# Alternating 512-column and 256-column products in a TensorE-bound fp32r transformer kernel

## The reference, cut to what matters

```python
proj = jnp.einsum('bsd,dc->bsc', x, w_in[layer])
...
h = jnp.square(jax.nn.relu(jnp.einsum('bsd,df->bsf', x, w_ff1[layer])))
y = jnp.einsum('bsf,fd->bsd', h, w_ff2[layer])
...
a, b = jnp.split(x @ w_in, 2, axis=-1)
return (jax.nn.silu(a) * b) @ w_out
...
y_g = o_g.reshape(B, S, GDN_WIDTH_V) @ w_branch_gdn
```

## Time and profile before

| | |
|---|---|
| median of 3 runs | 1370.94 us (1370.84 to 1371.84) |
| span of the profiled execution | 1369.8 us |
| granted clock of TensorE, mean | 0.999 of full speed |
| matmuls, each with a weight load | 8592 |
| read from memory | 225.90 MB, 166 GB/s over the span |

### The profile page before, as it was taken

One profiled execution on the slowest core, in us unless ns is written; L12 is line 12 of the kernel. 1 busy time (PEld: TensorE's weight loads), 2 busy tenths in 40 slices (PEclk: granted clock), 3 DMA queues, 4 the chain that ended last, 5 costly groups with the idle time before them and its releaser, 6 DMA issues.

```text
span 1369.8 us, 24310 instructions
## 1 busy us (share of the span) xinstructions
PE 1355.6 (99%) x8592; PEld 1211.1 (88%) x8592; DVE 1045.3 (76%) x1622; ACT 801.3 (58%) x1310; POOL 23.3 (2%) x71
## 2 busy tenths in 40 slices
PE   8999999999999999999999999999999999999998
PEld 8888888989888888888899999999999998988886
DVE  5798888777666686666778888888888877666665
ACT  4445554644443364444668898898898853544444
POOL 6000000000000000000000000000000000000000
PEclk9999999999999999999999999999999999999999
DMA  8565554655556746666574453554543286666661
GB/s 265 153 193 155 150 147 153 201 196 190 184 191 197 226 137 202 184 184 186 153 199 117 131 154 99 146 144 112 141 130 122 82 213 203 173 207 197 187 184 62
DMA packets 291214, 227.80 MB, mean 166 GB/s; under 512 B 10882, under 2 KB 270164, under 8 KB 291156
## 3 DMA queue, kind: packets, MB, share of 16 engines
q1 hardware_dynamic: 291012, 226.75, 55.6%
q10 hardware_dynamic: 144, 0.26, 0.1%
HBM read 225.90 MB, written 1.08 MB: 166 GB/s over the span
## 4 chain that ended last, share of the span: by engine, by line
PE 93%; DVE 3%; ACT 1%; DVEq 1%; issue 1%; DMA 1%; ACTq 0%; SPq 0%
PE M L2066 10%; PE G L2066 9%; PE M L2054 7%; PE M L2055 7%; PE M L2056 7%; PE G L2049 5%; PE M L2068 5%; PE G L2051 5%; PE G L2050 5%; PE G L2068 5%; PE G L2188 2%; PE G L2940 2%; PE M L2749 1%; PE M L2767 1%; PE G L2054 1%; PE G L2056 1%
## 5 line engine op out<-in xcount | busy, mean ns | idle before, releaser
L1203 DVE TENSOR_TENSOR w_lo<-w_raw,w_hi 128x2048 fp32r<-128x2048 f32 (+2 forms) x249 | 481.3, 1936 | 132.4 <-ACT w_hi L647 128.1
L647 ACT ACTIVATE w_hi<-w_raw 128x2048 fp32r<-128x2048 f32 x198 | 377.9, 1909 | 169.4 <-PE M L2068 54.3
L2049 PE MATMUL G<-xa,w_hi 128*128 128x256 f32 x592 | 176.8, 299 | 0.0
L2051 PE MATMUL G<-xa,w_lo 128*128 128x256 f32 x592 | 167.2, 282 | 0.0
L2050 PE MATMUL G<-xa,w_hi 128*128 128x256 f32 x592 | 167.0, 282 | 0.0
L2066 PE MATMUL M<-xa,w_hi 128*128 128x512 f32 x600 | 151.5, 394 | 0.0
L2066 PE MATMUL G<-xa,w_hi 128*128 128x512 f32 x568 | 142.5, 393 | 0.0
L2066 PEld LDWEIGHTS M<-xa,w_hi 128*128 128x128 f32 x600 | 107.8, 189 | 19.8
L2066 PEld LDWEIGHTS G<-xa,w_hi 128*128 128x128 f32 x568 | 104.0, 188 | 21.3 <-issue 1.2
L2054 PE MATMUL M<-w_hi,xb 128*128 128x512 f32 x300 | 117.3, 391 | 0.0
L2055 PE MATMUL M<-w_lo,xb 128*128 128x512 f32 x300 | 117.1, 390 | 0.0
(11 more groups left out here) (446 smaller groups left out, 2540.6 us busy)
## 6 DMA issues: line engine op xcount, KB each, us to landing
w_raw<-in_w_in SPq DMA_DIRECT2D x150, 512.0 KB, 4.7
w_raw<-in_ffn_w_in SPq DMA_DIRECT2D x88, 512.0 KB, 5.1
w_raw<-in_w_ff SPq DMA_DIRECT2D x64, 512.0 KB, 4.2
w_raw<-in_ffn_w_out SPq DMA_DIRECT2D x44, 512.0 KB, 5.0
w_raw<-in_w_in SPq DMA_DIRECT2D x33, 256.0 KB, 3.2
w_raw<-in_w_out SPq DMA_DIRECT2D x16, 512.0 KB, 4.0
w_raw<-in_w_branch_gdn SPq DMA_DIRECT2D x16, 512.0 KB, 5.3
w_raw<-in_w_branch SPq DMA_DIRECT2D x12, 512.0 KB, 4.2
```

Source lines behind the costliest of these rows:

```text
L647: nc.scalar.activation(w_hi[:, slot, :], w_raw[:, slot, :], ACT.Copy).then_inc(hi_ready, 1)
L1203: return v.tensor_tensor(dst, src, hi.bitcast(F32), ALU.subtract)
L2049: mm(out_, w[0], x[0], start=first, stop=False)
L2051: return mm(out_, w[1], x[0], start=False, stop=last_)
```

## The change

In both places the second loop over the k-tiles goes, and its product moves into the first loop. For each k-tile, the 512-column product with `w_hi` is followed at once by the 256-column product with `w_lo`. The operands, the banks, the start and stop flags and the signal on the last product are the same.

```diff
@@ -2064,7 +2064,6 @@
                 both_parts = bank.rearrange("p (h t) -> p h t", h=2)
                 for k in range(KT):
                     mm(both_parts, wh[:, k, at:at + P], xa[:, :, k, :], start=k == 0, stop=False)
-                for k in range(KT):
                     ins = mm(bank[:, 0:T], wl[:, k, at:at + P], xa_hi[:, k, :], start=False, stop=k == KT - 1)
             ins.then_inc(gemm_done, 1)
@@ -2938,7 +2937,6 @@
             wl_ = w_lo[:, c % RING, :].rearrange("p (k c) -> p k c", c=P)
             for k in range(16):
                 mm(G[:, n % 2, :].rearrange("p (h t) -> p h t", h=2), wh[:, k, :], xb[:, :, k, :], start=k == 0, stop=False)
-            for k in range(16):
                 ins = mm(G[:, n % 2, 0:T], wl_[:, k, :], xb_hi[:, k, :], start=False, stop=k == 15)
             ins.then_inc(gemm_done, 1)
```

## The result

The changed kernel takes 1377.08 us (median of four runs, 1376.63 to 1377.52) against 1371.15 for the kernel before on the same chip: a ratio of 1.0043, with an interval of 1.0031 to 1.0055. It is slower by 6 us, twice what a measurement can just tell apart. The profiled span went from 1369.8 to 1375.8 us, at the same granted clock of 0.999.

A forecast was written before the change was run, and what follows sets the result against it. TensorE's matmul stream was taken as the bound. Gains of 2.28, 0 and 0.15 us made 2.4, less 0.4 lost in the attention loop: 2.0 us, giving 1368.9 us; range 1362 to 1376, the forecast's own 1367 to 1370.

The forecast's parts named there:

- the price of the pair: TensorE's stream: a 512- and a 256-column product in turn cost their steady prices, 226.7+120 = 346.7 ns.
- 32 x 0: Groups of eight pairs directly behind 512-column products, 32 of 146: alternation gains nothing, 2.77 us either way.
- 8 x -19: Eight sixteen-pair groups of lines 2940/2942: 5.547 us instead of 5.566, a gain of 19 ns each.
- long groups: The eight sixteen-pair groups of lines 2940/2942, expected to read 5.55 us each after the change.
- 114: Groups of eight pairs not directly behind 512s: 2.773 us instead of 2.793, 20 ns gained each, 2.28 us in all.
- The 384/128 pairs: Attention lines 2390 and 2391, 287 ns a pair: taken as evidence that the surcharge goes with the load, not width changes.
- The upper bound: Highest price of an alternating pair: 232 for a never-settled 512 plus 120 for a 256, 352 ns.
- Rival 3: TensorE's stream never settles in alternation: 351 ns a pair, 1374.5 us, or 1375.5 at 352; chance 0.20.
- One load ahead: TensorE's weight loads: each starts with the product before it, so one load is ahead, under exactly one product.
- rival 1: Runs of 256 are bound by their weight loads, so alternation costs 340 ns a pair: 1360.0 us; chance 0.17.
- The run of 512s that follows a swiglu group keeps its slow start: Products behind a swiglu group start behind a 256 either way; their first five should still take 1.16 us.
- The attention loop was to lose half of its gain: Forty groups in the attention loop: half of their 0.8 us gain, 0.4 us, counted as lost there.

The follow-up runs named there:

- short loads: Changed kernel with wide products' weight loads cut to 64 of 128 columns from the second k-tile on: 1362.88 us; the same cut in the kernel before: 1371.99 us.
- the bench: Kernel before with its 13 equal feed-forward chunks each given another order or width; alternating chunk 5.640 us, runs of eight 5.559 us.
- the spacers: Kernel before with 13 alternating feed-forward chunks, each behind one extra narrow product of 16 to 256 columns; whole chunks 5.61 to 5.73 us.

## Why the prediction was wrong

**The step that failed** is the price of the pair: "I therefore take 226.7+120 = 346.7 ns a pair, the steady prices." In 142 of the 154 groups the pair settled at 353.3 ns: eight pairs took 2.830 us behind other groups of a step and 2.810 behind 512s, not 2.773 and 2.77. In the feed-forward, with 13 of each, that is 13 x 44 + 13 x 37 ns = 1.05 us more, as measured. The 512s and 256s do have a cycle in which the steady prices add up: twelve groups ran in it, at 346.7. But it is not the only one, and the prediction had no row that said which of them the stream would take.

The whole sum, term by term: in place of 32 x 0 stand 32 x 44 ns = 1.41 us, and in place of 8 x -19 the long groups' 8 x 87 = 0.70. The "114" hold 87 groups that do stand behind 256s, at +31 ns in the mean in place of -20 (2.71 us), and 27 that stand behind small products, which the prediction priced like the others; they took 2.85 to 3.06 us before, and +17 now (0.45). Together that is 5.27 us.

**The evidence for it was read too far.** The 384/128 pairs have a short product as the narrow one, so the wide product waits openly for its load, and the rest of the pair looked like one surcharge per load. That said nothing of a narrow product whose columns take nearly as long as the load, nor of a stream with more than one steady cycle.

**The upper bound was too low.** 352 was built from 232 for a 512, the mean of the five slow ones. The starts behind those rows already held single products of 228 to 236; 236 and 120 would have given 356 as an upper end, 1380.7 us in the prediction's own sum, and a range that held the result. (The cycle of three has 240 or 241 in it.) Rival 3, at 0.20, had the direction and the place right, a stream that never gets to the steady prices; but it does settle, into an exact cycle, and the price of 351 to 352 was too small by 1 to 2 ns a pair.

**What held.** TensorE's stream is the bound, at 99% and 97% of the chain; its waits stayed at 7.2 us; the clock stayed at 0.999. Which half of the bank the 256s go to costs nothing, as priced. One load ahead, under one product, was read rightly for these products. "The load of the next 512 still has only the 256 to hide under" stood in the text against rival 1; the short loads show that this load's length counts, and the forecast did not ask what it would do to its own price.

**What held in part.** "The run of 512s that follows a swiglu group keeps its slow start": in the feed-forward, yes (24 products in 5.467 us, unchanged); behind swiglu groups, no (5.503 against 5.467). There 32 pairs end at another point of the cycle of three than 16 pairs do, and ten products instead of five pass until the stream settles. In 18 runs that is 0.65 us that no step had. The attention loop was to lose half of its gain; it cost 0.78 us instead. Ten of its 40 groups did get the forecast price, 346.7; the eight in the chunk that all four turns share took 12 to 16 ns less than before. The long groups were to read 5.55; they read 5.65.

**What stays open.** The load of the next 512, 112 ns at its own pace, under a 256 that needs 107 to 120, takes part in the price: cutting it is shown to help, in the whole kernel as on the bench. That it alone makes the alternation dear is not shown. With the whole load, alternation was no dearer than the settled prices beside products of 480, 448 and 384 columns, nor behind three of the spacers. What in TensorE makes the cycles 340, 346.7, 350 or 353.3 ns long, and why a spacer of 112 columns leads to another one than 96 or 128, was not settled; no run here looks inside.

## What to carry to other kernels

Read prices from start to start, and use a settled price only for the order in which it was measured: in another order the stream can lock into a dearer cycle, and what ran ahead can choose it. For 512 and 256 columns long runs were the cheapest order measured; for 448 and 256 alternation was cheaper than runs, so no rule for other widths follows. Test another order on one loop with a dozen equal chunks before it is put in everywhere. As a bound for an unmeasured order, take the dearest single product of a disturbed stretch, not its mean.

## What was not expected of the hardware

- An alternating stream runs in exact cycles of one, two or three pairs (346.7 ns a pair for one and two, 353.3 for three), repeated to 1 ns over 16 and 32 pairs; whether one product of 16 or of 128 columns stands ahead of it decides between them.
- With the wide product at 448 columns and all loads whole, alternation cost 5.165 us a chunk and runs of eight 5.205; at 512 columns it was 5.640 and 5.559.
- Identical groups one behind the other took 2.72 and 2.80 us (wide load of 112 columns).
- Sixteen more columns in the narrow product cost 0.017 us a chunk in alternation and 0.100 in runs; sixteen fewer won 0.165 and 0.087.
- A shorter weight load can make a run slower: wide loads of 64 columns cost 18 ns a chunk in runs of eight.
- What a product costs on top of its columns at 2.4 GHz is not quite one surcharge: in runs of eight, 512 and 480 columns settled at 226.7 and 213.3 ns, 13.3 over their columns, but 448 and 384 at 203 and 177, some 17 over.
